# Three extra products per unit in the looped head groups of prompt attention

## The reference, cut to what matters

```
logits = jnp.einsum('bqkgd,bskd->bkgqs', qg, k.astype(f32)) * (HEAD_DIM ** -0.5)
...
p = jax.nn.softmax(jnp.where(causal, logits, -jnp.inf), axis=-1)
o = jnp.einsum('bkgqs,bskd->bqkgd', p.astype(v.dtype), v)
```

## Time and profile before

| what | value |
|---|---|
| time, median of 3 runs | 1813.83 us (1812.87 to 1815.3) |
| time of the profiled execution | 1814.97 us |
| its span on the core | 1813.1 us |
| looped groups of layer 0 | 272 to 427 us of the span, some 52 us a group |
| looped groups of layer 1 | 1094 to 1228 us of the span, some 45 us a group |
| TensorE busy over the span | 1606.7 us, 89% |
| mean granted TensorE clock | 0.918 of full speed |

### The profile page before, as it was taken

The page is one execution under the profiler, slowest core; times in us unless marked ns, Lnnn a source line. Parts: engine busy times, 40 slices in busy tenths (PEclk is TensorE's granted clock), DMA queues, the critical chain, the costliest instruction groups (busy, mean ns, idle before and its releaser), DMA issues.

```text
span 1813.1 us, 30957 instructions
## 1 busy us (share of the span) xinstructions
PE 1606.7 (89%) x12193; PEld 1431.5 (79%) x12193; DVE 802.3 (44%) x1731; ACT 675.1 (37%) x1210; POOL 143.7 (8%) x273
## 2 busy tenths in 40 slices
PE   4598958889888999999899888999898999998996
PEld 3485447777567999999799777778497999998995
DVE  0234967777334433333444524443335334334443
ACT  2433313445223433333433444445225333333334
POOL 0312001111100000000000131111101000000000
PEclk9698668889889999999999898889898999999998
DMA  6515830002441355445323031002642222222301
GB/s 187 178 41 166 286 132 24 23 0 116 174 148 51 117 186 163 153 146 179 115 75 101 4 132 46 23 0 117 221 128 70 88 86 86 90 81 75 100 30 47
DMA packets 154361, 189.81 MB, mean 105 GB/s; under 512 B 6741, under 2 KB 148221, under 8 KB 149974
## 3 DMA queue, kind: packets, MB, share of 16 engines
q1 hardware_dynamic: 143906, 144.72, 25.1%
q0 software_dynamic: 5600, 36.44, 5.4%
q10 hardware_dynamic: 4768, 7.42, 1.3%
HBM read 183.92 MB, written 4.83 MB: 104 GB/s over the span
## 4 chain that ended last, share of the span: by engine, by line
PE 72%; DVE 12%; issue 8%; ACT 5%; DMA 2%; another core or an unknown queue 1%; DVEq 0%; ACTq 0%; POOL 0%; SPq 0%; POOLq 0%
PE ps L529 51%; PE ps L1155 3%; PE ps L1224 2%; DVE arena L1137 2%; PE ps L1206 2%; PE ps L553 2%; DVE small L1136 1%; PE ps L1174 1%; PE ps L612 1%; DVE arena L1388 1%; PE ps L1445 1%; PE ps L1499 1%; PE ps L1215 1%; DMA const<-in_const 1%; ACT arena L1290 1%
## 5 line engine op out<-in xcount | busy, mean ns | idle before, releaser
L529 PE MATMUL ps<-hH,wH 128*128 128x260 f32 x2576 | 531.7, 288 | 55.5 <-DVE hL L680 36.2
L529 PE MATMUL ps<-hH,wL 128*128 128x260 f32 x2576 | 526.2, 286 | 0.0
L529 PE MATMUL ps<-hL,wH 128*128 128x260 f32 x2576 | 525.7, 286 | 0.0
L529 PEld LDWEIGHTS ps<-hH,wH 128*128 128x128 f32 x2576 | 405.6, 192 | 63.7 <-issue 62.8
L513 DVE TENSOR_TENSOR wL<-ring,wH 128x1024 fp32r<-128x1024 f32 (+1 forms) x170 | 203.2, 1199 | 549.4 <-ACT wH L507 549.3
L507 ACT ACTIVATE wH<-ring 128x1024 fp32r<-128x1024 f32 (+1 forms) x182 | 188.4, 1037 | 583.5 <-PE ps L529 570.2
L529 PEld LDWEIGHTS ps<-hH,wL 128*128 128x128 f32 x2576 | 404.5, 192 | 0.0
L529 PEld LDWEIGHTS ps<-hL,wH 128*128 128x128 f32 x2576 | 404.4, 192 | 0.0
L1290 ACT ACTIVATE arena<-arena 128x128 f32<-128x128 f32 (+3 forms) x128 | 72.2, 564 | 189.1 <-DVE arena L1374 103.3
L1206 PE MATMUL ps<-arena 80*128 (+4 forms) x256 | 103.7, 498 | 6.8 <-DVE arena L1271 2.6
L1224 PE MATMUL ps<-arena 128*128 (+1 forms) x640 | 91.8, 277 | 14.3 <-ACT arena L1298 13.9
(11 more groups left out here) (267 smaller groups left out, 1785.5 us busy)
## 6 DMA issues: line engine op xcount, KB each, us to landing
ring<-in_w_ada SPq DMA_DIRECT2D x48, 1024.0 KB, 7.8
ring<-in_w_up SPq DMA_DIRECT2D x44, 1024.0 KB, 5.1
ring<-in_w_down SPq DMA_DIRECT2D x16, 1024.0 KB, 5.4
ring<-in_w_in_a SPq DMA_DIRECT2D x8, 1024.0 KB, 7.5
ring<-in_w_down SPq DMA_DIRECT2D x8, 768.0 KB, 4.6
ring<-in_w_in_b SPq DMA_DIRECT2D x6, 1024.0 KB, 5.4
ring<-in_w_o_a SPq DMA_DIRECT2D x4, 1024.0 KB, 7.7
ring<-in_w_o_b SPq DMA_DIRECT2D x4, 1024.0 KB, 10.2
```

Source lines behind the costliest of these rows:

```text
L529: ins = pe.matmul(ps[:, 2 * p + half, 0:HT], w[:, h, kc, t * P:t * P + P], mov[:, k0 + kc, half * HT:half * HT + HT], start=(first and kc ...
```

## The change

In the looped groups (where `nxt` is not None), from unit 2 on, TensorE's step gets three products `pe_beat` ahead of the transposes, and the two waits there change places: first the wait on at_pt, then the three products, then the wait on at_p. A product of `pe_beat` takes 128 columns of hH as weights and 256 columns of hH as the moving operand, and writes 128 x 256 results into the bank that the unit's transposes overwrite next. Units 2 to 15 have them, that is steps 4 to 17 of each of three groups in each of two layers: 14 x 3 x 2 = 84 places, 252 products. Nothing is taken out.

```
+        def pe_beat(pe, bank, n):
+
+            for _ in range(n):
+                pe.matmul(ps[:, bank, 0:PC], hH[:, 0, 0:P], hH[:, 1, 0:PC], start=True, stop=True)
...
                 v = u - 2
                 if 0 <= v < NU:
                     qt = v // GR
-                    pe.wait_ge(S("at_p"), n * NU + (v + 1))
                     if v >= 2:
                         pe.wait_ge(S("at_pt"), n * NU + (v - 1))
+                        if nxt is not None:
+                            pe_beat(pe, 2 + v % 2, 3)
+                    pe.wait_ge(S("at_p"), n * NU + (v + 1))
                     for kb in range(qt + 1):
                         ins = pe.transpose(ps[:, 2 + v % 2, kb * P:kb * P + P], Pr[:, v % 2, kb * P:kb * P + P], ident)
```

## The result

The changed kernel takes 1826.37 us (median of 4 runs, 1825.98 to 1828.51) against 1814.57 us before in the same comparison; the ratio is 1.0069, interval 1.0051 to 1.0086. That is 9 to 16 us slower, 11.8 by the medians. The forecast was 1842 with a range of 1828 to 1852: the direction holds, the size is less than half. The profiled execution took 1828.51 us, with a span of 1826.7.

A forecast was written before the change was run, and what follows sets the result against it. TensorE, busy 89% of the span, was taken as the bound. Per group 4.81 us in layer 1 and 4.75 in layer 0, three groups each, made 28.7 us: 1842 us forecast, range 1828 to 1852.

The forecast's parts named there:

- The price of a set: Array time of three added products, read from group 3's unread products: 0.42 us, or 0.75 us in a cold stretch.
- my lower bound of 24.5 us: All six groups with a set at 0.36 us, 0.72 cold, from the projection's 0.12 us spacing; 1838 us in all.
- Step 9 of layer 0: Set hidden in the rotation's 2.6 us wait, costing 0; step 10 behind it still cold, 0.75 us.
- the clock holds over the rotation's wait: Rival, layer 0 step 9: the set keeps the clock up, 12.7 us back, about 1830 us; chance 0.12.
- A sign of being wrong: Named as refuting the forecast: products at steps 9 to 11 of layer 0 run at the upper clock.
- Cover in layer 1: Waits for ScalarE's copy hide 0.56 us of steps 7 to 9's sets and all of steps 15 and 16's.
- the stages behind attention swallowed nothing: Answers a rival: the sample stage's wait for gathered caches hides the delay, time stays at 1814 us; chance 0.02.

The follow-up runs named there:

- Experiment 4: Against the kernel before: none of the change's products, 14 unread products at step 9 of layer 0's looped groups, ahead of the rotation's wait; ratio 0.9946.
- 2 and 3: The change in one layer only, against the kernel before: layer 0 alone, 126 products, ratio 1.0004; layer 1 alone, 126 products, ratio 1.0045.
- experiment 9: Only layer 0's sets of three products at steps 7, 8 and 9, against the kernel before; ratio 0.9965.
- 6: Only layer 0's set at step 9, 9 products in all, against the kernel before; ratio 0.9986 (0.9971 to 1.0001).
- 7: Against the kernel before: no product of the change, 8 unread products once ahead of layer 0's loop; they fell into a wait there; ratio 0.9997.
- the kernel of 11 and 12 that leaves step 9 out: Against the kernel before: unread products only where TensorE waits in looped groups (steps 2, 3, 16, 19, layer 1's step 8), none at step 9; ratio 0.9940.
- experiment 11: Against the kernel before: unread products only where TensorE waits in both layers' looped groups, including 20 at layer 0's step 9; 1800.14 us, ratio 0.9922.
- experiment 1: Only the two waits change places, no product added, against the kernel before; ratio 0.9998 (0.9989 to 1.0007).

## Why the prediction was wrong in size

The way was right: the products stand behind the scores in steps where TensorE is full, no exponential was late, and they cost. The sum was 28.7 us, the two traces give 2.8 + 9.8 = 12.6 us over the six groups. Three steps of the prediction make the difference, and the second is the largest.

**The price of a set: mis-sized.** I took 0.42 us and a cold 0.75, it is 0.36 and 0.65. Through the same steps my lower bound of 24.5 us was the one to take, 4.2 us less. The row of four unread products from which I took 0.14 us each stands behind a wait in the code (`pe_keys`), and in the trace a row behind a wait is some 0.1 us longer, once. The same four value products of layer 1, first with nothing awaited (to 1155.58 in the earlier trace rows), then behind a wait (from 1157.06 in the earlier trace rows):

```profile
1155.19 0.56 PE L1224 MATMUL ps<-arena 128*128 x4
...
1157.55 0.39 PE L1233 MATMUL ps<-const,arena 128*128 128x128 f32 x2
```

0.39 us and 0.49 us. With 0.1 off, the four unread products take 0.46 in place of 0.56, or 0.12 each; that this wait explains their row is my reading, and the 0.36 us a set is measured without it. The estimate that I made from the Trainium skill, TensorE: Matmul & The Clock Gate, section Back-to-back issue gap, whose formula is for an isolated product, was 0.33 us a set; it is closer than my reading of the row, and still below the measured 0.36.

**Step 9 of layer 0: the wrong rival preferred.** I costed the clock as unmoved and gave "the clock holds over the rotation's wait" 0.12. It held, in one group wholly and in two in part, and layer 0 lost 2.8 us where the sets at 0.36 us would have made 12.1. The 9.3 us between them answer to the 19 us less at the lower level, of which some two thirds lie around this wait. That rival's own sum, 12.7 us back, taken from the lower bound of 24.5, would have given 11.8; I had set it against 28.7. That this meets the measured 11.8 is luck: by layers it is 12.4 and -0.6 us, where 9.8 and 2.8 were measured. My argument against it, that over 2 us of idleness stay and the set stands ahead of them, was wrong: 2.29 us stayed, and the clock held or fell for a shorter time. A sign of being wrong that I had named, products at steps 9 to 11 of layer 0 at the upper clock, is what the second group shows. Experiment 4 shows that the clock at this wait pays, 2 and 3 that layer 0 is where the change got it back; which part of the change keeps the clock up is not settled. The sets of steps 7, 8 and 9 together did so (experiment 9), that of step 9 alone did not in its trace (6), and groups without any of them held in part as well (7, and the kernel of 11 and 12 that leaves step 9 out). The Trainium skill, TensorE: Matmul & The Clock Gate, section HAM oscillation — how this bites in real kernels, says that gaps let the clock fall and steady work holds it. Here the rows agree, experiment 11 (1.00 through layer 1) most of all, though with waits of 2.29 to 2.65 us, shorter than the gaps of its example.

**Cover in layer 1: somewhat more.** At 0.36 us a set my steps give 12.4 us, measured are 9.8, 0.9 us less a group. From the starts of the scores in the first group, before against after: step 4 costs 0.45 us (forecast 0.72 by the lower bound; its set took 0.65, but the clock rose 0.2 us of work earlier), steps 5 and 6 0.72, steps 7 to 9 0.20 (0.52: step 9's own wait and the restarts behind both waits covered too), steps 10 to 14 1.64 (1.80), steps 15 and 16 nothing, step 17 0.36, and 0.14 us comes back by the next group's first value product.

The rest held. The exchange of waits is free (experiment 1), and the stages behind attention swallowed nothing. The whole change stayed on the slow side because its sets lie mostly in full steps: in layer 1 no wait at which the clock turns got one.

## What to carry to other kernels

Unread products paid here where the engine stood still and the clock fell, if they filled most of the wait, and cost their full array time where it was full; so list its waits, place by place, before placing them. When pricing a new instruction from a row, check whether that row starts behind a wait, and read its time from the next row that follows without a gap. Where a change touches a stretch in which the clock falls, price the clock by itself, and add its gain to each price bound instead of to the likeliest one alone.

## What the runs showed that I had not expected

A cut of the idle stretch from 2.65 to 2.29 us, with two fuller steps ahead of it, went with a clock around it of 0.83 or 1.00 in place of 0.66; the same cut alone left it at 0.66 and 0.67 in the profiled execution. How these two share in it, and whether the wait's place in time has a part, stays open: the runs that were to shift it did not. Neither is needed: filling the waits at a group's end and start alone, without step 9, also gave most of the gain (0.9940 against 0.9922), and the clock around the rotation's wait was 0.83 in all three groups, though the wait was 2.65 us as before and steps 4 to 9 of layer 0 had no product added. By what way, no run isolates; the second group:

```profile
342.00:352.00 10.00, 9.53 (x56) 8.06 (x57) 6.48 (x22) 2.17 (x6) 0.00 (x0) 0.83 0.00 0
```
